# Fixed pairs of experts with their weights loaded once a layer, and expert output rows scattered to memory and summed at the layer's end, in a two-layer hybrid step on one core

## What is computed

```python
def _moe(h, router_w, router_b, w_gate, w_up, w_down):
    B, T, D = h.shape
    tok = h.reshape(B * T, D)
    scores = jax.nn.sigmoid(jnp.dot(tok, router_w).astype(jnp.float32))
    biased = scores + router_b.astype(jnp.float32)
    grp_score = jnp.sum(lax.top_k(biased.reshape(-1, N_GROUPS, GROUP_SIZE), TOP_K)[0], axis=-1)
    best = jnp.argmax(grp_score, axis=-1)
    in_grp = (jnp.arange(N_EXPERTS) // GROUP_SIZE)[None, :] == best[:, None]
    _, idx = lax.top_k(jnp.where(in_grp, biased, -jnp.inf), TOP_K)
    w = jnp.take_along_axis(scores, idx, axis=-1)
    w = w / jnp.sum(w, axis=-1, keepdims=True)
    gates = jnp.sum(jax.nn.one_hot(idx, N_EXPERTS, dtype=jnp.float32) * w[..., None], axis=1)
    act = jax.nn.silu(jnp.einsum('nd,edf->nef', tok, w_gate)) * jnp.einsum('nd,edf->nef', tok, w_up)
    out = jnp.einsum('nef,efd->nd', act * gates[..., None].astype(act.dtype), w_down)
    return out.reshape(B, T, D).astype(h.dtype)
...
    x = _layernorm(ALPHA * x + gate2 * f, ln_g[l, 1], ln_b[l, 1])
```

## Time and profile before

| | |
|---|---|
| median of 3 runs | 2161.76 us (2159.8 to 2167.05) |
| the profiled execution | 2165.28 us, of which its span 2163.4 us |
| mean granted clock of PE in it | 0.962 of 2.4 GHz |
| busy, share of the span | PE 91%, PEld 47%, DVE 44%, ACT 20%, POOL 10% |
| DMA | 421.47 MB, mean 195 GB/s |
| expert stages | about 776 to 1047 us and 1801 to 2133 us |

### The profile page before, as it was taken

The page is one execution under the profiler, slowest core; times in us unless marked ns, Lnnn a source line. Parts: engine busy times, 40 slices in busy tenths (PEclk is TensorE's granted clock), DMA queues, the critical chain, the costliest instruction groups (busy, mean ns, idle before and its releaser), DMA issues.

```text
span 2163.4 us, 22048 instructions
## 1 busy us (share of the span) xinstructions
PE 1966.0 (91%) x7969; PEld 1026.3 (47%) x7969; DVE 949.4 (44%) x1952; ACT 424.7 (20%) x803; POOL 206.0 (10%) x218
## 2 busy tenths in 40 slices
PE   6999999989999879999799999998999988999994
PEld 3546766444444444333354676644444444433331
DVE  1637757646343342211753775764601133222126
ACT  1131151141001311111223115114100131111011
POOL 2123320000000000000002332000000000000000
PEclk7999999999999979999899999998999998999997
DMA  9421020453536379999532102044342337999993
GB/s 325 119 80 40 1 93 6 175 171 121 190 121 233 119 283 421 421 421 421 194 94 72 40 1 93 6 175 167 126 155 91 143 140 288 421 421 421 421 421 143
DMA packets 109563, 421.47 MB, mean 195 GB/s; under 512 B 6802, under 2 KB 7170, under 8 KB 78640
## 3 DMA queue, kind: packets, MB, share of 16 engines
q1 hardware_dynamic: 101072, 393.49, 47.8%
q0 software_dynamic: 8416, 26.98, 3.7%
HBM read 413.10 MB, written 7.34 MB: 194 GB/s over the span
## 4 chain that ended last, share of the span: by engine, by line
PE 63%; DMA 19%; DVE 10%; ACT 4%; issue 2%; SPq 1%; POOL 0%; DVEq 0%; POOLq 0%; ACTq 0%
PE bank L452 23%; DMA s_gla<-in_exp_w_up 17%; PE bank L623 6%; PE bank L575 6%; PE bank L897 6%; PE bank L984 6%; PE bank L639 2%; PE bank L1005 1%; PE bank L490 1%; PE bank L1019 1%; PE bank L795 1%; PE bank L805 1%; PE bank L852 1%; DMA ring<-in_w_mod 1%; DMA qkvp<-token_rows,row_index 1%
## 5 line engine op out<-in xcount | busy, mean ns | idle before, releaser
L452 PE MATMUL bank<-ring,xt_gla 128*128 128x512 f32 x1248 | 542.7, 595 | 10.1 <-ACT shared L1582 5.5
L452 PEld LDWEIGHTS bank<-ring,xt_gla 128*128 128x128 f32 x1248 | 236.6, 191 | 306.7 <-issue 304.3
L984 PE MATMUL bank<-ring,shared 128*64 128x512 f32 x960 | 223.5, 606 | 10.1 <-DMA ring<-in_exp_w_gate 10.0
L2195 DVE TENSOR_TENSOR shared<-shared,bank 128x512 f32<-128x512 f32 x20 | 21.2, 1061 | 350.9 <-PE bank L984 350.9
L984 PEld LDWEIGHTS bank<-ring,shared 128*64 128x64 f32 x960 | 95.2, 139 | 119.3 <-issue 74.6
L1005 PE MATMUL bank<-xt_gla,shared 128*64 128x512 f32 x320 | 141.5, 596 | 0.0
L623 PE MATMUL bank<-shared 128*128 128x128 f32 x1024 | 128.2, 281 | 10.1 <-DVE shared L1884 8.9
L623 PEld LDWEIGHTS bank<-shared 128*128 128x128 f32 x1024 | 121.3, 191 | 22.9 <-DVE shared L1884 15.0
L575 PE MATMUL bank<-xt_gla,ring 128*128 128x384 f32 x384 | 124.3, 487 | 2.4 <-DVE xt_gla L1679 2.4
L897 PE MATMUL bank<-ring,qkvp 128*128 128x512 f32 x288 | 124.7, 593 | 0.0
L1019 PE MATMUL bank<-shared 128*128 128x512 f32 x240 | 111.3, 601 | 1.6 <-ACT shared L1616 1.6
(11 more groups left out here) (372 smaller groups left out, 2412.1 us busy)
## 6 DMA issues: line engine op xcount, KB each, us to landing
ring<-in_exp_w_gate SPq DMA_DIRECT2D x80, 1024.0 KB, 24.3
ring<-in_w_in SPq DMA_DIRECT2D x32, 2048.0 KB, 10.4
ring<-in_w_mod SPq DMA_DIRECT2D x24, 2048.0 KB, 8.1
ring<-in_exp_w_up SPq DMA_DIRECT2D x40, 1024.0 KB, 24.1
xt_gla<-in_exp_w_down SPq DMA_DIRECT2D x40, 1024.0 KB, 23.3
s_gla<-in_exp_w_up SPq DMA_DIRECT2D x20, 1024.0 KB, 26.9
qkvp<-in_exp_w_down SPq DMA_DIRECT2D x20, 1024.0 KB, 21.8
xt_gla<-in_exp_w_up SPq DMA_DIRECT2D x20, 1024.0 KB, 24.9
```

Of the source, the lines that this page charges most:

```text
L452: mm = pe.matmul(ps[:, 0:width], xtv[:, k, t * P:(t + 1) * P], w_of(k), start=(k == 0), stop=(k == KC - 1))
L984: mm = pe.matmul(ps[u * SLOTS:(u + 1) * SLOTS, :], xg[:, at:at + SLOTS], w[u][:, k, :], start=(part == k == 0), stop=(part == 1 and k == 3))
```

## The change

- **Pairs.** A turn takes experts i and i+2 of a group (`PAIR_EXPERTS`), always both. A pair takes as many passes as its fuller expert needs at 64 tokens a pass; all passes of a pair follow one another. The list now holds, for every pass, its pair's experts, the first token place and the pair's number, and for each pair its last pass. There are at least 8 passes a layer.
- **Loads.** SP walks over the 8 pairs instead of the turns, and loads a chunk of the next pair when the present pair's last pass has used it. POOL waits for the chunk's DMA and tells PE with a semaphore of its own, once for each pass.
- **Rows.** The products with `hott` and the additions into `yacc` leave the loop. ACT multiplies an output row by its gate as it copies it, and POOL scatters the 128 rows of a turn by indirect DMA to a tensor in memory, `expert_rows`: 384 rows for a token's first choice, 384 for its second, and 128 that empty slots write to. All but the last turn of a layer go this way; the last turn still goes through `hott` and PSUM.
- **The end of a layer.** SP waits for the scatters and loads both halves, 6 transfers of 128 x 1024; DVE adds them and goes on as before.
- **Preparation.** The rows of `expert_rows` are cleared once, by two DMAs of 3 MB that SP issues in layer 0 after POOL has cleared `s_gla`; POOL scatters one narrow row of zeros first, so that the semaphore's count starts right. The clear of `yacc` (line 2153) goes, and the router works out each row's place (`homes`).

The core of the diff:

```diff
-JOBS = E + MORE + 2
-PAIRS_MAX = (E + MORE) // 2
+PAIRS_MAX = E // 2 + MORE
+TURNS = PAIRS_MAX + 2
+PAIR_EXPERTS = tuple((g * 4 + i, g * 4 + i + 2) for g in range(NG) for i in range(2))
...
                 def chunk(q, j):
 
-                    pe.wait_ge(sem(f"expert_chunk{j}_in"), (q + 1) * 32)
+                    pe.wait_ge(sem(f"expert_chunk{j}_ready"), q + 1)
...
-                    added(pe, n, 2)
+                    out_empty(pe, n)
                     output(n)
                     used(pe, "gather", n + (l + 1), 1)
                     slots(n + 2)
-                    added(pe, n, 3)
+                    used(pe, "gate", n)
                     hidden(n + 1, "gate", 0)
-                    added(pe, n, 0)
-                    back(n, lambda k: None, range(3))
-                    added(pe, n, 4)
                     hidden(n + 1, "up", 2)
-                    added(pe, n, 5)
                     used(pe, "slots", n + (l + 2))
                     gather(n + 2)
                     turned(n + 1)
...
-                    back(n, bank_wait, range(3, 2 * T))
...
+                    if l == 0 and n == 3 * RING:
+                        sp.wait_ge(sem("state_zeroed"), 1)
+                        for i in range(DEPTH):
+                            sp.dma_start(expert_rows[i][P:, :].rearrange("(r p) d -> p r d", p=P), fan(s_gla[:, 0:D], 6))\
+                                .then_inc(sem("rows_zeroed"), 16)
...
-                with sp.Fori(0, turns) as i:
-                    n = i + before
-                    experts = [sp.value_load(jobs[0:1, bass.ds(i * 2 + (W_AT + 2 + u), 1)], min_val=0, max_val=E - 1)
-                               for u in range(2)]
+                for pair in range(1, E // 2):
+                    end = sp.value_load(jobs[0:1, LAST_AT + pair - 1:LAST_AT + pair], min_val=pair - 1, max_val=PAIRS_MAX - 2)
                     for j in range(6):
-                        pair_used(j, n)
+                        pair_used(j, end + before)
                         for u in range(2):
-                            load_part(l, j, u, experts[u])
+                            load_part(l, j, u, PAIR_EXPERTS[pair][u])
                 last = turns + before
+                rows_sent(sp, l, last)
+                for t in range(T):
+                    for k, to in enumerate((yacc[:, t, :], second[t])):
+                        at = P + k * TOK + t * P
+                        sp.dma_start(to, expert_rows[l][at:at + P, :]).then_inc(sem(f"expert_sum{t}_in"), 16)
...
+                def ready(j, pairs):
+
+                    pool.wait_ge(sem(f"expert_chunk{j}_in"), (pairs + l * E // 2) * 32)
+                    pool.sem_inc(sem(f"expert_chunk{j}_ready"), 1)
...
                 with pool.Fori(0, turns) as i:
                     n = i + before
+                    now, then = (pool.value_load(jobs[0:1, bass.ds(i + (P_AT + at), 1)], min_val=1, max_val=E // 2 + at) for at in range(2))
+                    for j in (4, 5):
+                        ready(j, now)
+                    for j in (0, 1):
+                        ready(j, then)
                     made(pool, "gather", n + (l + 1), 1)
                     rows(n + (l + 2))
+                    out_empty(pool, n + 1)
+                    pool.sem_inc(sem("expert_rows_sent"), 1)
+                    pool.indirect_dma_start(expert_rows[l], bass.IndirectOffsetOnAxis(row_home[:, :], 0), oe, None)\
+                        .then_inc(sem("expert_rows_out"), 16)
+                    for j in (2, 3):
+                        ready(j, then)
...
-                def output_in(q):
+                def output_in(q, weight):
+                    rows_sent(act, l, q)
                     for half in range(2):
                         ps, free = made(act, "out", q, half)
-                        act.activation(oe[:, half * W5:(half + 1) * W5], ps[:, :], ACT.Copy).then_inc(free, 1)
+                        act.activation(oe[:, half * W5:(half + 1) * W5], ps[:, :], ACT.Copy, scale=weight).then_inc(free, 1)
...
                 def back_set(q):
 
                     dve.wait_ge(sem("slots_kept"), q + (l + 1))
-                    dve.tensor_scalar(hott, c("slots"), slot_now[:, 0:1], slot_now[:, 1:2], ALU.is_equal, ALU.mult)\
-                        .then_inc(sem("expert_back_set"), 1)
+                    out_empty(dve, q)
+                    rows_sent(dve, l, q)
+                    dve.tensor_copy(slot_used, slot_now)
+                    dve.tensor_tensor(row_home[:, :], slot_now[:, 2:3], c("token")[:, 0:1], ALU.max).then_inc(sem("expert_back_set"), 1)
...
-                    add(n)
                     back_set(n + 1)
                     slots_kept(n + 2)
...
                 for t in range(T):
+                    dve.wait_ge(sem(f"expert_sum{t}_in"), 32 * (l + 1))
+                    link(dve.tensor_tensor(yacc[:, t, :], yacc[:, t, :], second[t], ALU.add))
                     link(dve.tensor_tensor(yacc[:, t, :], yacc[:, t, :], gatev[:, min(t, 1), :], ALU.mult))
                     link(dve.scalar_tensor_tensor(out=xv[:, t, :], in0=xv[:, t, :], scalar=ALPHA, in1=yacc[:, t, :], op0=ALU.mult, op1=ALU.add))
```

More of the change, by code:

```diff
@@ L1026, in _ @@
                 used(pe, "gather", before + l, 1)
+                hidden(before, "gate", 0)
                 slots(before + 1)
-                hidden(before, "gate", 0)
                 hidden(before, "up", 2)
@@ L1628, in _ @@
                     turned_in(n + 1)
-                output_in(turns + before)
+                output_in(turns + before, 1.0)
                 centre(l, 1)
@@ L2207, in _ @@
                 link(ins)
[L2208 removed]
+                pick(before, PAIR_EXPERTS[0], (0, 0))
                 slots_in(before + l)
@@ new lines, in _ @@
+                pair, first, base = (otok[0:1, 2 * W5 + TURNS * (E // 2 + at):2 * W5 + TURNS * (E // 2 + at + 1)] for at in range(3))
+                idx = c("slots")[0:1, 0:TURNS]
+                by_pair = mor.rearrange("p (g u i) -> p g u i", g=NG, u=2)
+                link(dve.tensor_tensor(passes.rearrange("p (g i) -> p g i", g=NG), by_pair[:, :, 0, :], by_pair[:, :, 1, :], ALU.max))
+                link(dve.tensor_scalar(passes, passes, 1.0, None, ALU.add))
+                link(dve.tensor_tensor_scan(ends, c("ones")[0:1, 0:E // 2], passes, 0.0, ALU.mult, ALU.add))
@@ new lines, in _ @@
+                link(dve.tensor_tensor(past, fan(ends, TURNS), wide(idx, E // 2), ALU.is_le))
+                link(dve.tensor_reduce(pair, past, AX.X, ALU.add))
+                link(dve.tensor_reduce(first, past.rearrange("p n (a b) -> p n a b", b=2)[:, :, :, 1], AX.X, ALU.add))
+                link(dve.scalar_tensor_tensor(out=first, in0=first, scalar=2.0, in1=pair, op0=ALU.mult, op1=ALU.add))
+                link(dve.tensor_tensor(past, past, fan(passes, TURNS), ALU.mult))
+                link(dve.tensor_reduce(base, past, AX.X, ALU.add))
@@ L2253, in _ @@
+                turns = turns_of(dve, l)
+                experts, first = turn_jobs(lambda table: slice(table + 1, table + 2))
+                pick(before + 1, experts, (first, first))
                 weigh(l, 1, l * 2)
-                turns = turns_of(dve, l)
                 slots_in(before + (l + 1))
@@ L2259, in _ @@
                     n = i + before
-                    experts, firsts = ([dve.value_load(jobs[0:1, bass.ds(i * 2 + (at + 4 + u), 1)], min_val=0, max_val=top)
-                                        for u in range(2)] for at, top in ((X_AT, E), (S_AT, TOK - SLOTS)))
-                    pick(n + 2, experts, firsts)
+                    experts, first = turn_jobs(lambda table: bass.ds(i + (table + 2), 1))
+                    pick(n + 2, experts, (first, first))
                     slots_in(n + (l + 2))
                     multiply(n + 1)
-                    add(n)
                     back_set(n + 1)
@@ L2278, in _ @@
                     for half in range(2):
-                        ps, free = made(dve, "back", last, 2 * t + half)
+                        ps, free = made(dve, "back", l, 2 * t + half)
                         dve.tensor_tensor(yacc[:, t, cuts[half]], gatev[:, min(t, 1), cuts[half]], ps[:, :], ALU.mult).then_inc(free, 1)
@@ L2283, in _ @@
                     for half in range(2):
-                        used(dve, "back", last, 2 * t + half)
+                        used(dve, "back", l, 2 * t + half)
                         link(dve.tensor_tensor(xv[:, t, cuts[half]], xv[:, t, cuts[half]], yacc[:, t, cuts[half]], ALU.add))
```

167 lines of the change are left out of this document (83 added, 84 removed).

## The result

| | before | after |
|---|---|---|
| median | 2164.41 us (4 runs) | 2135.01 us (4 runs, 2133.62 to 2144.23) |
| the profiled execution, its span | 2165.28, 2163.4 us | 2133.62, 2131.6 us |
| mean granted clock of PE | 0.962 | 0.957 |

The changed kernel takes 0.9874 of the time before, with a 95% interval of 0.9858 to 0.9891: 29.4 us less, where the prediction said 28.5.

A forecast was written before the change was run, and what follows sets the result against it. It took steady expert turns as transfer-bound, 31.12 us each, with PE close behind. -124.5 + 62.8 + 17.4 + 15.8 = -28.5 us, on the median of 2161.8, gave 2133 us; range 2106 to 2160.

The forecast's parts named there:

- Fewer loads: Expert stages: 8 pair loads a layer in place of 9 and 11; four steady periods of 31.12 us go, -124.5 us.
- Idle DMA time: Extra passes: held buffers leave the DMA engines dry for 10.8 us in layer 0, 10.8 and 41.2 in layer 1, +62.8 us.
- The scatters: Expert turns: 18 new transfers at 1.25 us, four of them free in idle stretches, +17.4 us, between 0 and 35.
- The landing of a scatter: Expert turns: the wait for a scatter to land is hidden; it binds from 15 us and decides from 22.
- the rival of 2177 us: Expert turns: the scatter's landing, some 24 us, sets the turn and makes the kernel slower, 2177 us; chance 0.11.
- The end of a layer: After the last output product: rows are read back and added before the combination, +7.9 us a layer, +15.8 in all.
- What costs nothing: Clearing the row buffers (14.9 us of DMA), the router's new DVE operations and the job list are hidden, no cost.
- The job list: Before the expert loop: a list of other length is hidden; were it not, 2 us a layer.
- A slower clock: Expert stages: PE, with gaps at every chunk, falls below full clock, +23 us, 2156 us; chance 0.11.
- theory A: For pairs loaded once without the scatter: only idle DMA time prices the extra passes, -48 us, about 2116 us.

The follow-up runs named there:

- scatter_alone: The changed kernel, but SP loads the weights anew for every pass; scatter, clearing and sums stay: 2198.33 us, ratio 1.0157 to the kernel before.
- thin_rows: The changed kernel, but the scatter writes only the first 16 of 1024 columns, to a narrow tensor of its own: 2109.87 us, ratio to before 0.9754.
- lean end: The changed kernel, but PE adds the second row tensor into PSUM for token tiles 1 and 2, and DVE scales once: 2126.63 us, ratio to before 0.9820.
- one_more: The changed kernel with one pass more, with empty slots, for the pair (4, 6) in both layers: 2162.88 us.
- pairs_alone: The kernel before with fixed pairs loaded once, but without scatter, clearing and sums: 2141.41 us, ratio 0.9899 to the kernel before.
- clear_twice: The changed kernel, but a second pair of row buffers, which nothing reads, is cleared ahead of the real ones: 2134.49 us, ratio to before 0.9859.

## Why the prediction was right, point by point

- **Fewer loads** (-124.5): 48 transfers fewer, at the rate and period expected. The net of loads and idle time was measured at -63.3 between scatter_alone and the changed kernel, and the sum had -61.7. That they lie so close is partly luck: the 124.5 holds four gathers that do not go, 5.0 us, and the 62.8 is 10.1 too high.
- **Idle DMA time** (+62.8): the stretches are where they were placed, and the two short ones have their length, 10.0 and 10.4 for 10.8. The long one has 32.3 for 41.2: the step that timed the successor's chunks with one gather in 31.1 us left out the rows of the extra passes, which hold up the last landing by 3.0 us (37.0 for 34.0) and fill 3.1 us of the stretch itself (1990 to 2000). The other 2.8 us are not traced. In all it is 52.7.
- **The scatters** (+17.4): 21.9 in the turns by thin_rows (the rest of its 25.1 belongs to the layers' ends). The price of one, 1.25 us, holds; that four lie free in idle stretches does not, nor did the sum count the gathers of the four turns whose periods it struck out (4 x 1.25 = 5). These 9.5 us and most of the 10 too many of idle time are one mistake seen from two sides: rows that move in the extra passes were counted as idle time. They cancel, and so the total came out nearer than its terms.
- **The landing of a scatter** hides, as said: 12.3 us at most, under the 15 from which it would bind, so the rival of 2177 us is out. The Trainium skill (DMA: Bandwidth & Descriptors, Queues, rings and completion order) has a DMA engine take the queues with work in turn; 11.0 us beside weight transfers of 26.63 and 28.00 agrees.
- **The end of a layer** (+7.9 each; the prediction's own 10.1 - 2.3 is 7.8): 9.1 - 2.3 = 6.8 us in layer 0 and 10.2 - 2.3 = 7.9 in layer 1. The lean end shows that it is on the path.
- **What costs nothing:** the clearing, shown. The job list was not tried.
- **A slower clock:** partly there, though the prediction named it as a sign of being wrong. Over the windows of the two stages the granted clock means 0.971 and 0.973, and 0.992 and 0.994 before. Transfer-bound turns swallow it, as the unchanged distances of 32.4 show; the first turn can cost 2.9 us, as in one_more. It did not come to 23 us; no run sets the clock apart from the rest, so its price is not measured.

With the measured terms the sum is -124.5 + 52.7 + 21.9 + 5 + 14.7 = -30.2, against -29.4 by the medians and -28.0 by the stages.

What the sum did not say is why the scatter pays at all. It priced the scatter's 5.35 us off PE only as a shorter idle time in the extra passes. pairs_alone shows what they are for: at 28.6 us a pass PE, not the transfers, sets every turn from the extra pass to the end of layer 0, and the same loads saved gain 23 us, where idle time alone (theory A) would have given 48.

## What to carry to other kernels

When a load is saved that the buffers cannot replace by the next one, the saving is the load less the time the DMA engines then run dry, and the engine that computes can become the bound: time both, and shorten that engine's pass. Count what moves in an idle stretch as traffic, not as idle time. Work that hid behind the old bound (here DVE's adds at the layer's end) has to be looked at anew: it was worth 8 us more.

## What the runs showed of the hardware

- A scatter of 128 rows of 4 KB lands 11.0 us (median) after its issue, and in 4.9 us where the DMA engines were otherwise idle (1993.69); with 64 bytes a row it still takes 7.8 (3.9 to 9.3). Most of the landing is not its bytes.
- Stores of 12.6 MB went out between the loads of the first projection, with the DMA engines at up to 421 GB/s in all (100 to 110 us of clear_twice), and delayed nothing that can be measured.
- After PE had waited 4 us for a gather, its next products ran at half speed in one_more (an output instruction took 1.11 us there, 0.64 in the changed kernel), and did not in the changed kernel after a wait of 3.5 us. The length of the wait alone does not tell the two apart: after 3.6 us the output instruction of thin_rows (layer 1) took 1.11 us, and after 3.7 us that of lean_end (layer 0) took 0.64.
